# Keys of the cache read token-minor from HBM in place of transposes on TensorE, in an encoder step for streams

## The reference

```python
def latent_attend(q_lat, q_rope, c, kr, w_uv, mask):
    s = (jnp.einsum('bqhk,bsk->bhqs', q_lat, c)
         + jnp.einsum('bqhr,bsr->bhqs', q_rope, kr)).astype(jnp.float32) * ATTN_SCALE
    ...
    p = jax.nn.softmax(s, axis=-1).astype(c.dtype)
    o_lat = jnp.einsum('bhqs,bsk->bqhk', p, c)
    return jnp.einsum('bqhk,khv->bqhv', o_lat, w_uv)
...
    c_all = jnp.concatenate([c_past.astype(c_new.dtype), c_new], axis=1)
    kr_all = jnp.concatenate([kr_past.astype(kr_new.dtype), kr_new], axis=1)
    o = latent_attend(q_lat, q_rope, c_all, kr_all, p['w_uv'], None)
```

## Time and profile before

| | us |
|---|---|
| median of 3 runs | 1944.83 |
| lowest and highest | 1942.0, 1945.01 |
| span of the profiled execution | 1942.6 |
| TensorE busy | 1912.8 (98%) |
| VectorE busy | 1061.3 (55%) |
| ScalarE busy | 767.2 (39%) |
| HBM traffic | 158.55 MB by DMA, mean 82 GB/s |

### The profile page before, as it was taken

How to read it: one execution, slowest core, us unless ns; L and a number is a source line. 1 busy time by engine, 2 the same in 40 slices (tenths; PEclk the granted TensorE clock), 3 DMA queues, 4 the chain that set the end, 5 groups by cost and what they waited for, 6 DMA issues and landing times.

```text
span 1942.6 us, 31496 instructions
## 1 busy us (share of the span) xinstructions
PE 1912.8 (98%) x11771; PEld 1807.6 (93%) x11771; DVE 1061.3 (55%) x1943; ACT 767.2 (39%) x1342; POOL 394.0 (20%) x322
## 2 busy tenths in 40 slices
PE   9999999999999999999999999999999999999998
PEld 9999999999987999999999999999999989988886
DVE  4354446445658612332366676666666677653632
ACT  4333233233322222211355555555555567761100
POOL 0221222122311010000042432432433410000000
PEclk9999999999999999999999999999999999999999
DMA  6121122022236312233211112111111253363521
GB/s 183 35 78 54 36 67 78 25 64 68 76 120 201 122 49 70 80 104 106 77 45 50 40 51 64 34 54 54 40 49 42 73 135 93 96 226 136 157 87 44
DMA packets 186082, 158.55 MB, mean 82 GB/s; under 512 B 36144, under 2 KB 170544, under 8 KB 185744
## 3 DMA queue, kind: packets, MB, share of 16 engines
q1 hardware_dynamic: 180784, 139.60, 23.7%
q10 hardware_dynamic: 5040, 17.37, 2.5%
q0 software_dynamic: 176, 0.43, 0.1%
HBM read 115.52 MB, written 41.84 MB: 81 GB/s over the span
## 4 chain that ended last, share of the span: by engine, by line
PE 54%; DVE 7%; issue 5%; ACT 3%; DMA 1%; DVEq 0%; ACTq 0%; SPq 0%
PE ps L115 16%; PE ps L117 16%; PE ps L116 16%; PE ps L1925 1%; PE ps L1908 1%; PE ps L1907 1%; DVE h_pt_l L109 1%; ACT h_p L2042 1%; DVE h_mx L2168 1%; DVE s_mx L2804 1%; DVE h_p L2125 1%; ACT h_p L2031 1%; DVE h_p L2130 1%; DMA m_g_raw<-scratch_o 1%; DVE h_gate L2190 0%
## 5 line engine op out<-in xcount | busy, mean ns | idle before, releaser
L1821 POOL TENSOR_SCALAR h_p<-h_p,h_rsum 128x128 f32<-128x128 f32 (+7 forms) x128 | 220.7, 1726 | 439.8 <-DVE h_rsum L2172 439.8
L115 PE MATMUL ps<-act_h,a_w_l 128*128 128x384 f32 x768 | 270.8, 353 | 1.6 <-DVE a_w_l L109 1.6
L117 PE MATMUL ps<-act_h,a_w_h 128*128 128x384 f32 x768 | 260.1, 339 | 0.0
L116 PE MATMUL ps<-act_l,a_w_h 128*128 128x384 f32 x768 | 259.8, 338 | 0.0
L115 PE MATMUL ps<-act_h,m_c_l 128*128 128x384 f32 x480 | 162.9, 339 | 0.0
L117 PE MATMUL ps<-act_h,m_c_h 128*128 128x384 f32 x480 | 162.6, 339 | 0.0
L116 PE MATMUL ps<-act_l,m_c_h 128*128 128x384 f32 x480 | 162.5, 339 | 0.0
L115 PEld LDWEIGHTS ps<-act_h,a_w_l 128*128 128x128 f32 x768 | 144.2, 188 | 6.4 <-issue 3.3
L116 PEld LDWEIGHTS ps<-act_l,a_w_h 128*128 128x128 f32 x768 | 144.4, 188 | 3.3 <-issue 3.3
L117 PEld LDWEIGHTS ps<-act_h,a_w_h 128*128 128x128 f32 x768 | 144.1, 188 | 0.0
L104 ACT ACTIVATE h_pt_h<-ps 128x128 fp32r<-128x128 f32 (+2 forms) x192 | 86.9, 489 | 106.6 <-PE ps L1925 106.4
(11 more groups left out here) (320 smaller groups left out, 4817.7 us busy)
## 6 DMA issues: line engine op xcount, KB each, us to landing
a_w_raw<-in_w_in_a SPq DMA_DIRECT2D x31, 512.0 KB, 4.0
m_c_raw<-in_w_in_b SPq DMA_DIRECT2D x20, 512.0 KB, 4.2
scratch_gate<-m_sg SPq DMA_DIRECT2D x16, 576.0 KB, 5.2
o_w_raw<-in_w_out_b SPq DMA_DIRECT2D x16, 512.0 KB, 6.5
h_gate<-scratch_gate SPq DMA_DIRECT2D x62, 128.0 KB, 2.1
scratch_og<-h_gate SPq DMA_DIRECT2D x62, 128.0 KB, 1.7
o_g_raw<-scratch_og SPq DMA_DIRECT2D x24, 256.0 KB, 4.0
a_xn<-in_x SPq DMA_DIRECT2D x9, 512.0 KB, 4.7
```

The costliest lines, as they stand in the source:

```text
L115: nc.tensor.matmul(out, ll, rh, start=first, stop=False)
L116: nc.tensor.matmul(out, lh, rl, start=False, stop=False)
L117: return nc.tensor.matmul(out, lh, rh, start=False, stop=last)
L1821: nc.gpsimd.tensor_scalar(weights_of(u), weights_of(u), rsum[:, u % PB], None, ALU.mult).then_inc(S["p_ready"], 1)
```

## The change

The host passes two more layouts of the caches (`cache_ckv_turned`, [sequence, 128, half, token]; `cache_krope_turned`, [sequence, 64, token]), and the kernel reads the keys from these. The cache in its old layout is still loaded, for the values. The key transposes of the sample stage and of `turn_first` are gone. A sequence's keys lie as 1040 columns in SBUF (raw data on the place of the low part) and are split there in three parts: latent half 0, latent half 1, rotary. The own tokens' rows are turned once, in the middle stage (`behind_gate` now takes tile 8 too), copied by ScalarE to `m_own`, stored by SP to `scratch_own` at j = 14, and loaded from there into columns 1024 to 1039 for each sequence, in pieces of 16 columns (64 bytes). SP waits for the scores of sequence i - 2 ahead of the key loads of sequence i, then for `cache_low` ahead of the cache load. Sequence 1's latents go to a buffer of their own, `own_raw`; its rotary keys are loaded when the last head pair is through. In the last head pair the first sequence's splits stand at units 12, 13 and at the end.

```diff
 def behind_gate(j):
     t = j - 3
-    return (t - 1 if 0 <= t - 1 < NPB else None), (t if 0 <= t < NT else None)
+    return (t - 1 if 0 <= t - 1 < NT else None), (t if 0 <= t < NT else None)
...
+            if j == HEADS - 2:
+                sp.wait_ge(th_k, NT)
+                sp.dma_start(d["scratch_own"], own[:]).then_inc(own_stored, 16)
...
             act.wait_ge(turned_k, t + 1)
+            if t == NT - 1:
+                nc.scalar.copy(own[:], b[:, 0:3 * P]).then_inc(th_k, 1)
+                return
...
-KEYS_FROM = 9
-NKT = 7
+KEYS_FROM = 12
+NKT = 3
...
-                if last and KEYS_FROM <= u < KEYS_FROM + NKT - 1:
-                    k.samples.turn_first(pe, u - KEYS_FROM)
...
-TURNS = ["W1", "W4", "W2", "W3", "K0", "K1", "K2", "K3", "K4", "K5", "K6", "W0"]
+TURNS = ["W0", "W1", "W4", "W2", "W3"]
...
+    def load_latent_keys(sp, i, par):
+        raw = latent_raw(i, par)
+        sp.dma_start(raw[:, :, 0:PAST], d["cache_ckv_turned"][bass.ds(i, 1)].rearrange("o p a s -> (o p) a s")).then_inc(ct_loaded[par], 16)
+        sp.dma_start(raw[:, :, PAST:KS], own(i)[:, 0:2]).then_inc(ct_loaded[par], 16)
+
+    def load_rotary_keys(sp, i, par):
         for copy in range(2):
+            sp.dma_start(kt_raw[par][copy * RD:(copy + 1) * RD, 0:PAST], d["cache_krope_turned"][bass.ds(i, 1)].rearrange("o e s -> (o e) s")).then_inc(kt_loaded[par], 16)
+        sp.dma_start(kt_raw[par][:, PAST:KS], own(i)[:, 2]).then_inc(kt_loaded[par], 16)
...
         def body(i, par):
+            sp.wait_ge(S["s_done"], i * 2 - 2)
+            load_latent_keys(sp, i, par)
+            load_rotary_keys(sp, i, par)
             sp.wait_ge(S["cl_ready"], i * NCP - NCP)
-            load(sp, i, par)
+            load_cache(sp, i, par)
+        sp.wait_ge(heads.S["pv_done"], PAIRS * NG)
+        load_rotary_keys(sp, 1, 1)
...
             pe.wait_ge(S["ql_ready"], i + 1)
+            pe.wait_ge(S["kl_ready"], i * NKT + NKT)
...
-            scores(i, par, 1, ["W3", "K0", "K1"])
-            values(i - 1, 1 - par, ["K2", "K3", "K4", "K5", "K6", "W0"])
+            scores(i, par, 1, ["W3", None, None])
+            values(i - 1, 1 - par, [None] * 5 + ["W0"])
...
+    def keys_high(act, i, par, j):
+        if j == 0:
+            act.wait_ge(ct_loaded[par], (i - par) * 16 + 32)
...
+        elif j == 2:
+            act.wait_ge(kt_loaded[par], (i - par) * 24 + 48)
+        raw, high, _ = keys_part(i, par, j)
+        round_high(nc, high, raw).then_inc(S["kh_ready"], 1)
...
+    def keys_low(dve, i, par, j):
+        dve.wait_ge(S["kh_ready"], i * NKT + (j + 1))
+        raw, high, low = keys_part(i, par, j)
+        round_low(nc, low, raw, high).then_inc(S["kl_ready"], 1)
```

More of the change, by code:

```diff
@@ L1067, in middle_programs @@
     kvg = late.take("m_kvg", [KVL])
+    own = late.take("m_own", [3 * P])
     bank = k.bank
@@ L1566, in _ @@
             before, now = behind_gate(j)
-            if before is not None:
+            if before is not None and before < NPB:
                 turned_low_latent(before)
@@ L2309, in samples_programs @@
     q_h, q_l = early.take("s_q_h", [2, 2, QS], F32R), early.take("s_q_l", [2, 2, QS], F32R)
-    kr_raw = early.take("s_kr_raw", [2, KB + 1, 2, RD])
+    own_raw = early.take("s_own_raw", [2, KS])
+    early.reserve(4 * (2 * (KB + 1) * 2 * RD - 2 * KS))
     c_raw1 = early.take("s_c_raw1", [KB + 1, KVL])
@@ L2330, in samples_programs, with turn_number @@
     names = ("q_loaded uv_loaded zeroed qh_ready ql_ready s_done masked max_done exp_done inv_done p_ready t_done t_high t_out "
-             "o_done o_out ch_ready cl_ready uv_done uv_out og_stored").split()
+             "o_done o_out ch_ready cl_ready kh_ready kl_ready uv_done uv_out og_stored").split()
     S = {n: m.sem("s_" + n) for n in names}
     c_loaded = [m.sem(f"s_c_loaded{i}") for i in range(2)]
[L2334 to L2349, removed]
+    ct_loaded = [m.sem(f"s_ct_loaded{i}") for i in range(2)]
+    kt_loaded = [m.sem(f"s_kt_loaded{i}") for i in range(2)]
+    def turn_number(i, x, par):
+        at = TURNS.index(x)
+        return i * len(TURNS) + at, 6 + (par + at) % 2
     def seqs(eng, body):
@@ L2446, in turn_bank @@
         return bank[:, at]
-    def turn_keys(pe, j, b, par):
-        what, a, s0, w = step_of_keys(j)
-        if what == "new":
-            for x in range(2):
-                nc.tensor.transpose(b[:, x * P:x * P + P], c_raw[par][:, KB, x * P:x * P + P], k.ident[:])
-            mm = nc.tensor.transpose(b[:, 2 * P:3 * P], kr_raw[:, par, KB].rearrange("p a b -> p (a b)"), k.ident[:])
-        else:
-            for x in range(w):
-                src = c_raw[par][:, s0 + x, a * P:a * P + P] if what == "c" else kr_raw[:, par, s0 + x].rearrange("p a b -> p (a b)")
-                mm = nc.tensor.transpose(b[:, x * P:x * P + P], src, k.ident[:])
-        mm.then_inc(S["t_done"], 1)
-    def turn_first(pe, j):
-        if j == 0:
-            heads.bank_free(pe, 1)
-            pe.wait_ge(c_loaded[0], 32)
-        else:
-            pe.wait_ge(S["t_out"], j)
-        if j == 4:
-            pe.wait_ge(kr_loaded[0], 64)
-        turn_keys(pe, j, bank[:, 1], 0)
-    block.turn_first = turn_first
     @block.tensor
@@ L2708, in body @@
                 k.output.group_high(act, 0)
-            for x in ("K0", "K1"):
-                high(x, i, par)
+            else:
+                keys_high(act, i + 1, 1 - par, 0)
             exp(i, 1)
-            high("K2", i, par)
+            if not last:
+                keys_high(act, i + 1, 1 - par, 1)
             normed(i, 1)
-            for x in ("K3", "K4"):
-                high(x, i, par)
             if not last:
+                keys_high(act, i + 1, 1 - par, 2)
                 q_high(act, i + 1, 1 - par)
-            high("K5", i, par)
             cache_high(act, i, par, 2)
-            high("K6", i, par)
             if last:
@@ L2779, in low @@
         def low(x, i, par):
-            if isinstance(i, int) and i < NSEQ and x not in turns(i):
-                return
-            n, at = turn_number(i, x)
+            n, at = turn_number(i, x, par)
             j = int(x[1])
-            if x[0] == "K":
-                return keys_low(dve, j, n, at, 1 - par)
             b = bank[:, at]
@@ L2848, in body @@
                 k.output.row_low(dve, 0)
-            for x in ("K6", "W0"):
-                low(x, i, par)
+            low("W0", i, par)
         seqs(dve, body)
         for x in BEFORE:
-            low(x, NSEQ, 0)
+            low(x, NSEQ - 1, 1)
     def gate_values(dve):
```

189 lines of the change are left out of this document (72 added, 117 removed).

## The result

| | before | after |
|---|---|---|
| median of the runs, us | 1943.67 (4 runs) | 1964.39 (1963.31 to 1965.22, 4 runs) |
| ratio, 95% interval | | 1.0107 (1.0096 to 1.0119) |
| span of the profiled execution | 1942.6 | 1963.3 |
| mean granted clock | 0.998 | 0.988 |

The change makes the kernel slower by 20.7 us. The forecast was 1949, with a range that ended at 1961. Its direction was right; the size was five times too small.

A forecast was written before the change was run, and what follows sets the result against it. TensorE and the ScalarE/VectorE split chain were taken as level, the chain binding after the change. Terms summed to +4.0 us: 1942.6 to 1946.6 profiled, with 2.2 for the runs' median about 1949; range 1944.0 to 1961.0.

The forecast's parts named there:

- middle stage: Three added transposes for the own tokens cost at most 0.4 us; taken as +0.4 us.
- last head pair: Seven transpose blocks (2.96 us) fall out, two longer splits enter; bounds 0 and -3.6, taken as -2.0 us.
- start of the stage to T1, loads with it: Sample stage's start to sequence 1's T: 22.7 us becomes 20.0, so -2.7; loads add +0.5.
- T1 to T2: Sequence 1 to 2 in the sample stage: 20.2 us becomes 21.3, ScalarE running late there; +1.1.
- T2 to T6: Four steady sequences of the sample stage: 78.66 us becomes 83.7; +5.0.
- T6 to T7: Sequence 6 to 7 in the sample stage: 19.2 us becomes 20.9; +1.7.
- What bounds the kernel: Sample stage: TensorE's 19.3 us and the ScalarE/VectorE split chain are level; removing TensorE work helps only if the chain shortens.
- What is removed, what a split costs: Key transposes worth 2.96 us a sequence, 23.7 for eight; 1040-column splits take 1.07 us on ScalarE, 1.24 on VectorE.
- The chain walked: Steady sequence: splits, maximum, exp, normalising and queries let scores start at T + 11.45; TensorE idles 4.5 us.
- From the start of the scores to T: TensorE's scores part of each steady sequence's period, taken as 9.48 us of the 20.9.
- The clock falls in the new gaps: Rival: 1.2 GHz after two to five of six stalls, 2.6 us each; +5 to +13, 1954 to 1962; chance 0.30.
- Loads: Key loads mostly hidden; sequence 1's rotary keys delayed 0 to 3 us at the stage's start, taken as +0.5.

The follow-up runs named there:

- filled stall: The changed kernel plus 44 do-nothing identity transposes on TensorE behind the value matmuls of sequences 1 to 6, where it waits for the queries; 1951.94 us.
- without the own loads: The reordered kernel with two later moves (VectorE low halves, SP load order), then zeros for the 64-byte own-column loads in the last head pair; 1922.62 us.
- short pieces: The changed kernel with each key split cut into two of 520 columns, at the queue places of the kernel before's 512-column splits; 1947.32 us.
- one swap: The changed kernel with the maximum of query tile 1 moved ahead of the low half of keys part 0 on VectorE; 1949.41 us.
- reordered: The changed kernel with the same work in another order on ScalarE and VectorE: queries early, maximum ahead of all key splits; 1921.75 us.

## Why the prediction was wrong, point by point

The sum again, with T read off as before (T is the end of the second query tile's scores; sequence 4's is 1664.73 + 0.33). The points ahead of the stage are to be taken with care: one in the middle of the heads, with the same code ahead of it, lies between 1512.5 and 1514.8 in the executions of the variants, so the first row below is within that spread. The spread is mostly the clock again, in the wait of 2.5 us shown below: a gate multiplication in the heads starts at 1503.8 to 1504.8 in the seven executions in which it held there, and at 1505.6 to 1506.3 in the six in which it fell. It fell in both executions of this table.

| stretch | forecast | measured |
|---|---|---|
| middle stage | +0.4 | +0.43 |
| last head pair, to the first scores | -2.0 | +0.8 |
| start of the stage to T1, loads with it | -2.2 | -2.6 |
| T1 to T2 | +1.1 | +3.25 |
| T2 to T6 | +5.0 | +15.7 |
| T6 to T7 | +1.7 | +2.9 |
| behind T7 | 0 | +0.2 |
| sum | +4.0 | +20.7 |

- **What bounds the kernel.** Right. TensorE and the chain were level, removed work alone gave nothing, and the sign follows from that.
- **What is removed, what a split costs.** Right: the key transposes are gone, and the splits last 1.06 and 1.24 us where 1.07 and 1.24 were scaled.
- **The chain walked.** Right within 0.25 us at every point: keys part 0 to T + 1.96 (forecast 1.85), maximum to 3.33 (3.2), keys part 1 to 6.83 (6.6), normalising from 6.94 (6.8), keys part 2 to 10.35 (10.1), queries to 11.45 (11.3), scores from 11.68 (11.45), TensorE done at 6.9 (6.9). The kernel with the filled stall is this walk on its own, at a distance of 21.15 against 20.9.
- **From the start of the scores to T.** Here the step failed: this term of the period was taken as 9.48 us, from a row at the high clock, although the same walk put a stall of 4.5 us in front of it. Measured are 10.8 to 12.2, the more the longer the low level lasted (3.4 to 6.8 us). That is 1.3 to 2.8 us a sequence, 2.1 on average, and the filled stall gives back 12.6 over six.
- **The rival that had this.** "The clock falls in the new gaps" priced one stall at 2.6 us, in the right mechanism and somewhat high. It counted two to five of the six stalls, without a reason for leaving any out, and had only 0.30. The clock fell in all six: 12.6 us by the filled stall, 2.1 each. 1949 + 12.6 is 1961.6, and the 2.8 us of the last head pair, below, make up the rest. Six stalls at 2.6 us alone would have come to 1965 as well, with a price that is too high standing in for the heads.
- **What I read wrong.** "This trace's longest wait of TensorE is 2.5 us, and the slices show the higher level only." A slice is 48.6 us long and is shown in tenths. Looked at in stretches of 2 us, the kernel before shows the clock falling in just that wait, which ended at 597.33:

```profile
594.00:596.00 2.00, 0.81 (x8) 0.56 (x6) 1.17 (x2) 1.74 (x2) 0.00 (x0) 1.00 1.16 313
596.00:598.00 2.00, 0.67 (x2) 0.61 (x3) 1.97 (x4) 0.00 (x0) 0.00 (x0) 0.82 1.17 269
598.00:600.00 2.00, 2.00 (x6) 1.56 (x5) 1.92 (x5) 1.25 (x2) 1.06 (x2) 0.50 1.07 360
600.00:602.00 2.00, 2.00 (x9) 1.63 (x8) 1.74 (x4) 1.78 (x2) 0.00 (x0) 0.83 0.98 368
602.00:604.00 2.00, 2.00 (x10) 1.65 (x9) 2.00 (x2) 0.00 (x0) 0.00 (x0) 1.00 0.05 20
```

  One wait of 2.5 us, and 3.4 us at the low level, most of them behind it. With this answer the rival should have been the forecast, with all six stalls: each of 4.5 us, longer than that wait. The Trainium skill, TensorE: Matmul & The Clock Gate, Part 1, has the clock gated to the lower level when TensorE is idle. The traces agree for every wait of 2.9 us and more, and show no fall for those of 1.9 and less. Between these they go both ways: in this very wait, with the same code ahead of it and 2.4 to 2.75 us long, the clock fell in six of the 13 profiled executions and held in seven.
- **Last head pair.** Wrong, by 2.8 us. "Nearer the TensorE bound, since TensorE rarely waits before that end" is the sentence that failed. The stretch ends in three chains that were nearly level: VectorE's queue with the two long splits in it, the queries' landing, and TensorE. What I had named against the gain (the 0.5 us longer splits) was the smaller part; a fall of the clock in the 3.1 us wait added about 1.4 us (18 value matmuls in 3.6 us instead of 2.15).
- **Two readings of the queue before.** The prediction has four of the seven key splits behind the reciprocal, and five more blocks of transposes behind T. The order shown ahead of it has five splits there (K2 to K6), and TensorE's timeline six blocks (K1 to K6). The 6.9 us were worked out with six, so the sum does not change.
- **Loads.** The stated place, sequence 1's rotary keys, was harmless. The late ones were sequence 1's own columns (ScalarE waited 1.5 us) and the queries, 5 us later behind a blocked SP: the issue of a load behind a wait for a store was not followed through. The 64-byte pieces, against which I quoted the Trainium skill (DMA: Bandwidth & Descriptors, Specifications), cost nothing that the run without them shows in the last head pair; for the others, whose loads nobody waits for, it was not tried.
- **T6 to T7, T1 to T2.** As in the steady sequences: 1.7 and 1.1 were walked, and the filled stall, which has the walk without the clock, is shorter by 1.2 and 1.8 at these two places. Some 0.3 us of T1 to T2 is left without a cause.

## What to carry to other kernels

Before an edit is credited with time off TensorE, walk the chain that feeds it, and then price the clock in every gap that the walk opens: here a gap of 4.8 us cost 4.8 and another 2.1 on average. Read the granted clock in stretches of 1 or 2 us around the longest waits that the trace already has; a page's slices hide a fall of 3.4 us. One trace shows one outcome: the same wait kept the clock in some executions and lost it in others. And when work goes from TensorE, move what stands on the vector engines' queues in the same edit: the maximum ahead of splits that nobody needs yet, the splits into the waits for maximum and exp, the queries ahead of all. Where three engines and a load are level, taking from one shows the next.

## What the runs showed of the chip

- The granted clock fell from 1.00 to 0.50 in or just behind every wait of TensorE of 2.9 us and more (2.88 to 8.2 us, in eight of the kernels), and in none of 1.9 us and less. Between these the length does not decide: it fell with waits of 2.13 (without the own loads), 2.17 (short pieces), 2.7 (one swap) and 2.4 to 2.6 us (at 597 us, six executions), and held through waits of 2.12 (reordered), 2.66 (short pieces) and 2.4 to 2.75 us (at 597 us, seven executions).
- It need not fall in the wait. It fell 0.5 us after work had resumed at 1643.87 in the short pieces' kernel, and 1.3 us after it had at 1687.67 in that with one swap. It came back 3.4 to 6.8 us after it had fallen, and 10.2 in the run whose wait was 8.2 us, in each case while TensorE was working.
- Transposes that do nothing kept it up: with 44 of them in each stall of 4.8 us it stayed at 1.00 through the six, and the kernel was 12.5 us faster.
- With 2 to 5 MB issued ahead of it, a 128 KB store (median of its kind 1.7 us) let SP go on only 4.9 to 11.5 us behind its issue, and the small load of new rows for 16 partitions held SP for 4.1 to 8.1 us (4.5 in the kernel before, 0.8 where the queries were issued first). Leaving out the 64-byte pieces shortened neither.
